# One low part in four of the mixing stage made by ScalarE and an adding transfer instead of VectorE

## What is computed

```python
h = rmsnorm(x, norm_g)
proj = jnp.einsum('bld,dn->bln', h, w_in)
v, bg, cg, za, u, zb, ga, gb = jnp.split(proj, SPLITS, axis=-1)
ya = bg * causal_depthwise_conv_2(cg * v, conv_w)
ya = jnp.einsum('blc,cd->bld', ya * jax.nn.silu(za), w_out_a)
yb = jax.nn.gelu(s5_scan(u, ...))
```

## Time and profile before

| | us |
|---|---|
| median of 3 runs (2806.62 to 2811.38) | 2807.45 |
| the profiled execution's own time | 2807.17 |
| its span, first to last instruction | 2805.5 |
| busy of the span: TensorE matmul | 2708.0 (97%) |
| VectorE | 1963.6 (70%) |
| ScalarE | 1206.7 (43%) |
| GpSimd | 801.8 (29%) |

### The profile page before, as it was taken

The page is one execution under the profiler, slowest core; times in us unless marked ns, Lnnn a source line. Parts: engine busy times, 40 slices in busy tenths (PEclk is TensorE's granted clock), DMA queues, the critical chain, the costliest instruction groups (busy, mean ns, idle before and its releaser), DMA issues.

```text
span 2805.5 us, 48657 instructions
## 1 busy us (share of the span) xinstructions
PE 2708.0 (97%) x18906; PEld 2336.8 (83%) x18906; DVE 1963.6 (70%) x2305; ACT 1206.7 (43%) x1521; POOL 801.8 (29%) x548
## 2 busy tenths in 40 slices
PE   6999999999998999999999999989999999999998
PEld 4788988898897787888888888789898998888886
DVE  1377877787788677666666666699899899655554
ACT  2255455545545444333333333354333334543343
POOL 1066666676666510000000000002555552000000
PEclk8999999999999999999999999999999999999999
DMA  9866666676675676666666666545554555566664
GB/s 364 314 199 210 230 208 197 219 233 192 209 241 176 216 211 207 189 191 189 187 188 188 187 190 189 168 149 158 158 173 151 159 172 164 189 188 189 189 205 144
DMA packets 283916, 552.64 MB, mean 197 GB/s; under 512 B 16818, under 2 KB 54259, under 8 KB 282611
## 3 DMA queue, kind: packets, MB, share of 16 engines
q1 hardware_dynamic: 263632, 474.02, 54.7%
q0 software_dynamic: 19408, 76.06, 7.3%
q10 hardware_dynamic: 722, 0.28, 0.0%
HBM read 548.19 MB, written 2.10 MB: 196 GB/s over the span
## 4 chain that ended last, share of the span: by engine, by line
PE 82%; DVE 9%; ACT 4%; issue 2%; DMA 1%; SPq 1%; DVEq 0%; ACTq 0%; POOL 0%; PEld 0%
PE pg L1125 26%; PE pd L1125 18%; PE pg L819 13%; PE pg L1112 9%; PE pg L810 4%; PE pd L734 2%; DVE wl L2098 2%; DMA arena<-in_mod_w 1%; PE pg L838 1%; PE pd L999 1%; PE pd L981 1%; DVE arena L2430 1%; DVE arena L2432 1%; DVE arena L2425 1%; ACT arena L1484 1%
## 5 line engine op out<-in xcount | busy, mean ns | idle before, releaser
L2098 DVE TENSOR_TENSOR wl<-wr,wh 128x1024 fp32r<-128x1024 f32 x616 | 773.9, 1265 | 479.4 <-ACT wh L1604 476.0
L1604 ACT ACTIVATE wh<-wr 128x1024 fp32r<-128x1024 f32 x616 | 652.2, 1061 | 978.4 <-PE pg L1125 392.3
L605 POOL TENSOR_TENSOR wl<-wr,wh 128x1024 fp32r<-128x1024 f32 x195 | 480.5, 2465 | 400.6 <-ACT wh L1413 400.4
L1413 ACT ACTIVATE wh<-wr 128x1024 fp32r<-128x1024 f32 x216 | 227.7, 1057 | 347.6 <-PE pg L819 219.9
L1112 PE MATMUL pg<-hh,wh 128*128 128x256 f32 x1280 | 365.8, 286 | 3.1 <-DVE wl L2098 3.1
L1112 PE MATMUL pg<-hl,wh 128*128 128x256 f32 x1280 | 362.3, 283 | 0.0
L1112 PE MATMUL pg<-hh,wl 128*128 128x256 f32 x1280 | 361.8, 283 | 0.0
L1125 PE MATMUL pg<-wh,hh 128*128 128x512 f32 x832 | 327.3, 393 | 0.0
L1125 PE MATMUL pg<-wl,hh 128*128 128x512 f32 x832 | 326.3, 392 | 0.0
L1125 PE MATMUL pg<-wh,hl 128*128 128x512 f32 x832 | 325.4, 391 | 0.0
L819 PE MATMUL pg<-hh,wh 128*128 128x256 f32 x1024 | 301.2, 294 | 14.8 <-ACT arena L1461 12.0
(11 more groups left out here) (397 smaller groups left out, 5027.2 us busy)
## 6 DMA issues: line engine op xcount, KB each, us to landing
wr<-in_w_in SPq DMA_DIRECT2D x224, 512.0 KB, 3.9
wr<-in_ffn_w_gu SPq DMA_DIRECT2D x176, 512.0 KB, 4.3
wr<-in_gdn_w_in SPq DMA_DIRECT2D x128, 512.0 KB, 4.1
arena<-in_mod_w POOLq DMA_DIRECT2D x64, 1024.0 KB, 7.2
wr<-in_ffn_w_down SPq DMA_DIRECT2D x88, 512.0 KB, 3.9
arena<-in_mod_w SPq DMA_DIRECT2D x32, 1024.0 KB, 12.3
wr<-in_gdn_w_in SPq DMA_DIRECT2D x128, 256.0 KB, 3.0
wr<-in_gdn_w_out SPq DMA_DIRECT2D x56, 512.0 KB, 4.5
```

The source lines that it names most:

```text
L605: nc.gpsimd.tensor_tensor(wl[c % RING][:], wraw[c % 4], wh[c % RING][:].bitcast(F32), ALU.subtract)\
L1413: a(wh[c % RING][:], wraw[c % 4], ACT.Copy).then_inc(s_hi, 1)
L1604: a(wh[c % 4][:], wraw[c % 4], ACT.Copy).then_inc(s_hc, 1)
L2098: v.tensor_tensor(wl[c % 4][:], wraw[c % 4], wh[c % 4][:].bitcast(F32), ALU.subtract).then_inc(s_lc, 1)
```

## The change

For the 33 chunks with m = 1, 5, 9, ..., 129 (m counted from `CK_MIX`; all of them use the buffers number 1, `wh_58` and `wl_62` in the listings; the last is the second chunk of the next stage), VectorE no longer makes the low part. ScalarE writes the negated high part into `wl` right after the high part, and GpSimd issues a DMA that adds the raw weights from `wraw` onto it, both in SBUF. A new semaphore `s_ng` counts the negated parts, `s_la` the transfers (16 each). TensorE, and SyncE for the next load into the same `wraw`, wait for `s_la` where they waited for `s_lc`. The loops over the four passes are written out on SyncE and GpSimd.

```diff
+def by_dma(j, per, c):
+    m = absolute(j, per, c) - CK_MIX
+    return 1 <= m <= 129 and m % 4 == 1
+
+def lows(j, per, c):
+    if isinstance(j, int):
+        a = j * per + c
+        return a - max(0, min(33, (a - CK_MIX + 2) // 4))
+    return j * per + (c - 33 if c >= CK_GA else c)
...
         (SyncE, load)
-                sp.wait_ge(s_lc, j * per + (c + 1))
+                if by_dma(j, per, c - 4):
+                    sp.wait_ge(s_la, 4 * (absolute(j, per, c - 4) - CK_MIX - 1) + 16)
+                else:
+                    sp.wait_ge(s_lc, lows(j, per, c - 4) + 5)
                 sp.dma_start(wraw[c % 4], src).then_inc(s_w[c % 4], 16)
...
-            with sp.Fori(0, 4) as j:
+            for j in range(4):
                 for g, col in enumerate((C_V, C_CG, C_BG, C_ZA)):
...
         (GpSimd)
+            def low_by_dma(j, t):
+                slot = (CK_MIX + t) % 4
+                pool.wait_ge(s_ng, j * 8 + (t // 4 + 1))
+                pool.dma_start(wl[slot][:], wraw[slot], accum_op=ALU.add).then_inc(s_la, 16)
...
-            with pool.Fori(0, 4) as j:
-                restart()
+            for j in range(4):
                 for q in range(8):
+                    low_by_dma(j, 4 * q + 1)
                     if q % 4 == 0:
...
                     tables(j, q)
+            low_by_dma(4, 1)
...
         (TensorE, chunk and tchunk)
+            def ready(j, per, c):
+                if by_dma(j, per, c):
+                    pe.wait_ge(s_la, 4 * (absolute(j, per, c) - CK_MIX - 1) + 16)
+                else:
+                    pe.wait_ge(s_lc, lows(j, per, c) + 5)
...
-                pe.wait_ge(s_lc, j * per + (c + 5))
+                ready(j, per, c)
...
         (ScalarE, high)
                 a(wh[c % 4][:], wraw[c % 4], ACT.Copy).then_inc(s_hc, 1)
+                if by_dma(j, per, c):
+                    a(wl[c % 4][:], wraw[c % 4], ACT.Copy, scale=-1.0).then_inc(s_ng, 1)
...
         (VectorE, low)
+                if by_dma(j, per, c):
+                    return
```

More of the change, by code:

```diff
@@ L79, with absolute @@
 W_GDN = 128 * (NIT + 1)
+def absolute(j, per, c):
+    return j * per + c if isinstance(j, int) else c
+def by_dma(j, per, c):
[6 more added lines that the diff above has]
+    return j * per + (c - 33 if c >= CK_GA else c)
 def out_chunk(t):
@@ L396, in build @@
         s_lc = sem("s_lc")
+        s_ng = sem("s_ng")
+        s_la = sem("s_la")
         s_ck = sem("s_ck")
```

## The result

| | before | changed |
|---|---|---|
| median of the runs beside each other | 2809.41 (2806.62 to 2812.41, 4 runs) | 2833.93 (2829.66 to 2840.85, 4 runs) |
| the profiled execution's own time | 2807.17 | 2840.85 |
| its span | 2805.5 | 2839.2 |

The ratio is 1.009, its 95% interval 1.0077 to 1.0102: **24.5 us slower**, where 12 us faster had been forecast.

The account below looks back on a forecast made before the run. TensorE was taken to bound the kernel, with 17.6 us of its mixing-stage waits due to VectorE. 17.6 - 1.6 - 4.0 = 12.0 us less than 2807.17 gave 2795; range 2789 to 2850, the forecast case 2789 to 2802 (chance 0.52).

Parts of the forecast that it names:

- loop through buffer 1: Transfer landing, next load, ScalarE's copies, next issue: one turn 12.3 us per four chunks, hidden behind TensorE's 12.67.
- What bounds the kernel now: Mixing stage: TensorE bounds, waiting 17.6 us for VectorE; no more than about 18 us to be had.
- VectorE's part: Mixing stage: 33 low parts, 46.9 us, go; share falls from 92% to about 81%; 17.6 us on the path.
- I let most of them go: Of TensorE's 17.6 us of waits for VectorE, all vanish except about 0.4 us at four places, 1.6 us.
- ScalarE's part: 33 more copies of 1.0 us on ScalarE, busy 36%, lie beside other work and cost nothing.
- GpSimd's part: 33 more DMA issues, and tables waiting for the negated part, early by 0.6 us; charged 0.25 at 16 state-outs, 4 us.
- The issue of the transfer: GpSimd's issue of each adding transfer takes 0.77 us, 25 us more in all on an engine 55% busy.
- X: Time from issue to landing of the adding transfer: taken as 5.8 us; gain all given back at 6.75.
- Buffer 1's loop becomes the bound: Rival, chance 0.36: transfer too slow from 6.75 us, kernel slower; 2822 at 7.2, 2847 at 8, 2962 at 11.6.
- The wait changes its name: Rival: tables about 1 us late at every state-out give 16 us back, 2802 to 2812; chance 0.12 with the third.
- TensorE was never held by VectorE's low parts: Rival: only the pairs hold TensorE, so removing low parts frees nothing, 2807; counted with the second, together 0.12.

Follow-up runs that it names:

- the winning version: Changed kernel with each adding transfer issued behind the tables of its pair, only the stage's first one ahead of them: 2791.92 us beside 2810.21, ratio 0.9943.
- the kernel with the zeros between: Changed kernel with GpSimd writing zeros to its scratch, and waiting for that, between the transfer's issue and the tables: 2795.99 us, ratio 0.9948.
- late tables alone: Kernel before, with GpSimd waiting for the high part of chunk 4q + 1 ahead of pair q's tables, no transfer: 2834.18 us, ratio 1.0084.
- the thin one: Changed kernel with the transfer, still ahead of the tables, moving only 16 of 1024 values a partition: 2836.98 us, ratio 1.01.
- the kernel that holds the issue back: Changed kernel with the transfer behind the tables and its issue also waiting until pair q - 1 is done on VectorE: 2824.56 us, ratio 1.0056.

## Why the prediction failed

**The direction was wrong**: 2795 forecast, 2833.9 measured. The time lies inside the range by luck: the range had been stretched upward for the slow loop through buffer 1, which is not what happened.

- **What bounds the kernel now** held. The 17.6 us were there to be had: the winning version takes 18.3 us off, and its passes reach 101.4 against a floor of 101.3.
- **VectorE's part** held for what was removed (46.9 us forecast, 44.5 less in that group), and failed for what stayed: 81% became 88.7%, because the other instructions were taken to keep their durations. The step "I let most of them go" relied on that.
- **ScalarE's part** held: 33 copies of 1043 ns on average, and no wait of TensorE that names them.
- **GpSimd's part is the step that failed.** I charged 4.0 us for tables that come later, and asked only when they are *ready*: at 10.6 against 11.2. That held; no row of the change shows VectorE waiting for tables. I did not ask *what they run beside*. The earlier trace rows already had table operations at anything from 0.62 to 1.60 us beside VectorE's low parts, and I read this as scatter in GpSimd's finish, not as two engines that hold each other up. The reverse side of the same rows was VectorE's low part at 1421 ns on average, against the 1.23 us that one takes with GpSimd still (at 2183.01 in the kernel with the zeros between). Moved beside the pair, whose end TensorE waits for, that term is 24.6 us with all low parts on VectorE (late tables alone) and 11.6 with three in four.
- **The issue of the transfer**, in the same step, was charged as 0.77 us of GpSimd's own time; it took 0.89. That the tables directly behind it hold VectorE far longer, 26.5 us in all, stood in no row of before, since no DMA issue of GpSimd stands ahead of tables there.
- **The loop through buffer 1** was right in its form and did not decide. X was 4.6, under the 5.8 taken. The Trainium skill (DMA: Bandwidth & Descriptors, "Anatomy of one DMA — SWDGE (gpsimd) path") had given an estimate of 4.4, and the landing rows agree: minimum 4.5 and median 4.6 for the full transfer (one took up to 7.5), and 2.2 for the thin one, which by that section would be an estimate of about 2.0. The 7.2 of GpSimd's loads from HBM was the wrong neighbour.
- **The rivals.** "Buffer 1's loop becomes the bound" is refuted for the change (0.7 us of such waits) and shown for the kernel that holds the issue back. "The wait changes its name" came nearest in its place, a wait at each state-out, but had it at 16 us and by another way, tables not ready. "TensorE was never held by VectorE's low parts" is refuted: with the tables where they were, taking a quarter of the low parts away gives 14 to 18 us.
- **The clock** was in no term. The stage had stood at 0.99, with two short falls (to 0.68 and 0.57 over 4 us); the change has five, four of them with a stretch at 0.50, and 12 of its 33.7 us are there. So part of the cost of waits comes behind them.

## What to carry to other kernels

When an edit delays an operation that is itself off the critical path, cost it twice: when it is done, and beside what it runs until then. Durations of one operation that scatter in the profile (0.62 to 1.60 us) can mean that another engine is in it, as here, and the operation should then stay away from the few instructions that release the bottleneck. Put a GpSimd DMA issue behind GpSimd's operations rather than directly ahead of them; here one moved call was worth 33 us, and one more at the start 9.

## What the runs showed of the hardware

- **GpSimd's reads and VectorE's two-input operations hold each other up.** VectorE's subtraction of 256 values takes 424 ns with GpSimd still, about 640 beside table operations; its product of 1024 values 1225 and 1418 on average. A table operation of GpSimd takes 0.62 to 1.60 us. The Trainium skill (SBUF — State Buffer, "Who interferes with whom") says that a VectorE instruction with two SBUF inputs contends with a GpSimd one that reads SBUF and not with one that only writes it. These rows agree, and so does the writing of zeros beside the subtraction at 0.43 us.
- **A DMA issue of GpSimd makes this much worse for what runs behind it**: the subtraction has a median of 1794 ns, up to 2150, for the full transfer, 1801 for the thin one. It does so with table operations and with copies (1.31 us) that follow the issue without a gap, and not when 0.86 us of writing zeros lie between (at most 728), nor when nothing follows (0.42). In the timeline above the subtraction ends 0.3 us after the *second* table operation (GpSimd's times are rough). In six pairs of the change with two copies between issue and tables the subtraction begins about 1.9 us after the issue, takes 2.14 to 2.15 us and ends 0.3 us after the third operation that ran beside it. The Trainium skill (SBUF — State Buffer, "Summary: rules for kernel authors") says that of two such instructions the second to issue is blocked until the first finishes; here VectorE is held through two or three in a row, which is more. Why stays open: the runs separate the issue from the bytes moved and from what follows it, not what inside GpSimd does it. Longer gaps and other kinds of operation behind the issue were not tried.
- **An adding transfer within SBUF** of 512 KB, issued by GpSimd in 0.89 us, lands in 4.6 us (median), and in 2.2 us for 64 bytes a partition. In that stage the DMA engines moved 187 GB/s in all, transfers included, and 159 before.
